# A 16-expert block on one core: every other weight chunk of the expert ring is issued by ScalarE instead of SyncE

## The reference, cut to what matters

```python
gate, idx = lax.top_k(jnp.swapaxes(affinity, 1, 2), capacity)      # capacity 32
xe = jax.vmap(lambda hb, ib: hb[ib])(h, idx)
hidden = jax.nn.silu(jnp.einsum('becd,edf->becf', xe, w_gate)) * jnp.einsum('becd,edf->becf', xe, w_up)
ye = jnp.einsum('becf,efd->becd', hidden, w_down) * gate[..., None].astype(h.dtype)
```

## Time and profile before

| | |
|---|---|
| three runs, median (lowest to highest) | 1483.31 us (1483.19 to 1488.25) |
| profiled execution: its own time | 1483.69 us |
| profiled execution: span in the trace | 1482.0 us |
| busy: PE, PEld, DVE, ACT, POOL | 78%, 46%, 34%, 25%, 3% |
| mean granted TensorE clock | 0.874 of 2.4 GHz |
| bytes moved | 493.31 MB, mean 333 GB/s |
| chain that ended last | DMA 54%, PE 41%, DVE 4% |

### The profile page before, as it was taken

One profiled execution on the slowest core, in us unless ns is written; L12 is line 12 of the kernel. 1 busy time (PEld: TensorE's weight loads), 2 busy tenths in 40 slices (PEclk: granted clock), 3 DMA queues, 4 the chain that ended last, 5 costly groups with the idle time before them and its releaser, 6 DMA issues.

```text
span 1482.0 us, 19792 instructions
## 1 busy us (share of the span) xinstructions
PE 1151.1 (78%) x8185; PEld 685.5 (46%) x8185; DVE 503.4 (34%) x926; ACT 374.3 (25%) x618; POOL 41.5 (3%) x95
## 2 busy tenths in 40 slices
PE   9999999866666567567556666565666999999998
PEld 8887887321212212112112122122121788999887
DVE  6988895101101001011011010110110569665547
ACT  6658663101001000001000100000100364465434
POOL 2220120000000000000000000000000000000000
PEclk9999999987877877877787788788877999999999
DMA  8663528999999999999999999999999763555551
GB/s 305 199 251 110 193 86 351 391 426 429 425 427 428 427 429 427 428 428 428 428 429 428 429 428 427 429 427 427 429 428 428 267 213 137 177 174 196 189 186 52
DMA packets 58616, 493.31 MB, mean 333 GB/s; under 512 B 6666, under 2 KB 8260, under 8 KB 33988
## 3 DMA queue, kind: packets, MB, share of 16 engines
q1 hardware_dynamic: 57620, 491.54, 81.5%
q10 hardware_dynamic: 944, 1.05, 0.2%
HBM read 491.52 MB, written 1.05 MB: 332 GB/s over the span
## 4 chain that ended last, share of the span: by engine, by line
DMA 54%; PE 41%; DVE 4%; issue 1%; ACT 1%; DVEq 0%; POOL 0%; SPq 0%; ACTq 0%; POOLq 0%
DMA arena<-in_expert_w_down 15%; DMA arena<-in_expert_w_up 13%; PE ps L1860 13%; DMA arena<-in_expert_w_gate 12%; PE ps L1951 7%; PE ps L1865 6%; DMA ring<-in_expert_w_gate 5%; DMA ring<-in_expert_w_down 5%; DMA ring<-in_expert_w_up 4%; PE ps L2307 4%; PE ps L2325 2%; DVE w_split L1145 1%; PE ps L1930 1%; PE ps L2121 1%; PE ps L2152 1%
## 5 line engine op out<-in xcount | busy, mean ns | idle before, releaser
L1145 DVE TENSOR_TENSOR w_split<-ring,w_split 128x1024 fp32r<-128x1024 f32 (+3 forms) x178 | 200.8, 1136 | 99.8 <-ACT w_split L721 98.6
L2307 PE MATMUL ps<-ring,arena 128*32 128x512 f32 x1024 | 166.8, 795 | 84.9 <-DMA ring<-in_expert_w_up 60.4
L2307 PE MATMUL ps<-arena 128*32 128x512 f32 x1024 | 161.1, 770 | 88.3 <-DMA arena<-in_expert_w_up 59.9
L721 ACT ACTIVATE w_split<-ring 128x1024 fp32r<-128x1024 f32 (+3 forms) x178 | 175.4, 990 | 186.2 <-PE ps L1865 130.1
L1596 DVE TENSOR_TENSOR arena<-arena,ps 128x512 f32<-128x512 f32 x16 | 11.0, 688 | 494.2 <-PE ps L2307 494.2
L1603 DVE TENSOR_TENSOR xs<-ps,xs 128x512 f32<-128x512 f32 x64 | 39.8, 684 | 298.1 <-PE ps L2333 298.1
L2307 PEld LDWEIGHTS ps<-ring,arena 128*32 128x32 f32 x1024 | 33.8, 132 | 210.3 <-DMA ring<-in_expert_w_up 102.0
L2307 PEld LDWEIGHTS ps<-arena 128*32 128x32 f32 x1024 | 33.1, 128 | 209.6 <-DMA arena<-in_expert_w_up 97.5
L1951 PE MATMUL ps<-hT_hi,w_split 128*128 128x256 f32 x608 | 111.4, 284 | 0.1
L2325 PE MATMUL ps<-arena 128*32 128x256 f32 x1056 | 81.9, 462 | 37.2 <-DMA arena<-in_expert_w_down 34.2
L2325 PE MATMUL ps<-ring,arena 128*32 128x256 f32 x928 | 77.6, 492 | 39.7 <-DMA ring<-in_expert_w_down 37.5
(11 more groups left out here) (361 smaller groups left out, 1369.8 us busy)
## 6 DMA issues: line engine op xcount, KB each, us to landing
arena<-in_expert_w_gate SPq DMA_DIRECT2D x35, 2048.0 KB, 35.8
ring<-in_expert_w_up SPq DMA_DIRECT2D x35, 2048.0 KB, 36.0
ring<-in_expert_w_gate SPq DMA_DIRECT2D x29, 2048.0 KB, 36.2
arena<-in_expert_w_up SPq DMA_DIRECT2D x29, 2048.0 KB, 37.2
arena<-in_expert_w_down SPq DMA_DIRECT2D x25, 2048.0 KB, 34.5
ring<-in_expert_w_down SPq DMA_DIRECT2D x21, 2048.0 KB, 33.8
ring<-in_w_ff SPq DMA_DIRECT2D x32, 1024.0 KB, 4.9
ring<-in_w_in SPq DMA_DIRECT2D x24, 1024.0 KB, 5.0
```

The costliest lines, as they stand in the source:

```text
L721: act.activation(w_split[:, n % WBUFS, 0, 0:cols], slot_view(slot, cols)[:, n % 2, :], ACT.Copy).then_inc(split_hi, 1)
L1145: dve.tensor_tensor(buf[:, 1, :], w, buf[:, 0, :].bitcast(F32), ALU.subtract).then_inc(split_lo, 1)
L2307: m = pe.matmul(ps[j * CAP:(j + 1) * CAP, bank, :], xe[:, kt, :], w[:, r, j * FCOL:(j + 1) * FCOL], start=kt == 0, stop=kt == KT - 1, skip ...
```

## The change

`chunk_source` and `load_chunk` move out of SP's program, and `load_chunk` gets the issuing engine as an argument. Chunks with n >= 11 and n odd are issued by ACT, all others by SP as before; SP's waits for them are the same numbers as before. Since there are 12 chunks in an expert, odd n is odd k: ACT issues k = 1, 3, 5, 7, 9 and 11 of each expert, and so both parts of each k = 11. ACT issues them between its activations: 9 and 11 of this expert after L955's copy, 1 and 3 of the next after silu, 5 and 7 of the next after the copy of the hidden, each behind a wait of its own on `chunk_used`, with the same number as SP's. ACT's loop over 8 pairs becomes one over 6; the first and the last pair stand outside it. PE, DVE and POOL are unchanged.

```diff
+        def load_chunk(engine, slot, loaded, e, k):
+
+            source = chunk_source(e, k)
+            if k < EXPERT_CHUNKS - 1:
+                engine.dma_start(slot, source).then_inc(loaded, 16)
+                return
+            engine.dma_start(slot[:, 0:TAIL], source[:, 0:TAIL]).then_inc(loaded, 16)
+            engine.dma_start(slot[:, TAIL:WIDE], source[:, TAIL:WIDE]).then_inc(tail_loaded, 16)
+
+        def from_scalar(n):
+
+            return n >= SLOTS and n % 2 == 1
...
-            for n in T1_ORDER[2:] + tuple(range(SLOTS, PAIR * EXPERT_CHUNKS)):
+            for n in T1_ORDER[2:] + tuple(n for n in range(SLOTS, PAIR * EXPERT_CHUNKS) if not from_scalar(n)):
                 load_freed(n)
             with sp.Fori(1, EXPERTS // PAIR) as pair_i:
                 for n in range(PAIR * EXPERT_CHUNKS):
-                    sp.wait_ge(chunk_used, PAIR * EXPERT_CHUNKS * pair_i + n + 2)
-                    load_chunk(wide_slots[turn(n)], slot_loaded[turn(n)], pair_i * PAIR + n // EXPERT_CHUNKS, n % EXPERT_CHUNKS)
+                    if n % 2 == 0:
+                        sp.wait_ge(chunk_used, PAIR * EXPERT_CHUNKS * pair_i + n + 2)
+                        load_chunk(sp, wide_slots[turn(n)], slot_loaded[turn(n)], pair_i * PAIR + n // EXPERT_CHUNKS,
+                                   n % EXPERT_CHUNKS)
...
-            with act.Fori(0, EXPERTS // PAIR) as pair_i:
+
+            def load_odd(e, j_e, k, ahead, first):
+
+                n = EXPERT_CHUNKS * (j_e + ahead) + k
+                if first and n < SLOTS:
+                    return
+                act.wait_ge(chunk_used, slot_free(n) if first else EXPERT_CHUNKS * (e + ahead) + k + 2)
+                load_chunk(act, wide_slots[turn(n)], slot_loaded[turn(n)], e + ahead, k)
+
+            def expert(e, j_e, first=False, last=False):
+
+                act.wait_ge(scat_done, e + 2)
+                act.wait_ge(e_scatter, e + 1)
+                act.activation(scat, ps[:, 3, 256:512], ACT.Copy).then_inc(scat_ready, 1)
+                for k in (9, 11):
+                    load_odd(e, j_e, k, 0, first)
+                act.wait_ge(chunk_used, EXPERT_CHUNKS * e + T1_RELEASES + IN_CHUNKS)
+                act.wait_ge(hid_ready, e + 1)
+                act.activation(hid_g, ps[:, 0, :], ACT.Silu).then_inc(silu_done, 1)
+                if not last:
+                    for k in (1, 3):
+                        load_odd(e, j_e, k, 1, first)
+                act.wait_ge(hidT_done, e + 2)
+                act.activation(hidT, ps[:, 2, :].rearrange("p (c t) -> p c t", c=4), ACT.Copy).then_inc(hidT_ready, 1)
+                if not last:
+                    for k in (5, 7):
+                        load_odd(e, j_e, k, 1, first)
+                act.wait_ge(chunk_used, EXPERT_CHUNKS * e + T1_RELEASES + EXPERT_CHUNKS)
+                act.activation(ye, ps[:, 3, 0:DCOL], ACT.Copy).then_inc(ye_ready, 1)
+
+            for e in range(PAIR):
+                expert(e, e, first=True)
+            with act.Fori(1, EXPERTS // PAIR - 1) as pair_i:
                 for j_e in range(PAIR):
...
+                    expert(pair_i * PAIR + j_e, j_e)
+            for e in range(EXPERTS - PAIR, EXPERTS):
+                expert(e, e % PAIR, last=e == EXPERTS - 1)
```

More of the change, by code:

```diff
@@ L434, in hybrid_blocks, with chunk_source @@
         ENDS += [(len(CORNERS) - 1, CORNERS[-1][1], D - 512 + c, 256) for c in (0, 256)]
+        def chunk_source(e, k):
+            if k < 2 * IN_CHUNKS:
+                c = k % IN_CHUNKS
+                w = t["expert_w_gate" if k < IN_CHUNKS else "expert_w_up"][0, e]
+                return w[c * P * IN_ROWS:(c + 1) * P * IN_ROWS, :].rearrange("(p r) f -> p (r f)", r=IN_ROWS)
+            c = k - 2 * IN_CHUNKS
+            w = t["expert_w_down"][0, e]
+            return w[c * P * OUT_ROWS:(c + 1) * P * OUT_ROWS, :].rearrange("(p r) d -> p (r d)", r=OUT_ROWS)
+        def load_chunk(engine, slot, loaded, e, k):
[7 more added lines that the diff above has]
+            return n >= SLOTS and n % 2 == 1
         block = ctx.enter_context(nc.Block())
@@ L481, in _ @@
                               ).then_inc(small_loaded, 16)
[L482 to L490, removed]
             load(DENSE_SLOTS)
@@ L498, in _ @@
             sp.dma_start(router[:, :, :], t["router_w"][0].rearrange("(k p) e -> p k e", p=P)).then_inc(small_loaded, 16)
[L499 to L506, removed]
             def load_expert(n):
                 slot, loaded = expert_slot(n)
-                load_chunk(slot, loaded, n // EXPERT_CHUNKS, n % EXPERT_CHUNKS)
+                load_chunk(sp, slot, loaded, n // EXPERT_CHUNKS, n % EXPERT_CHUNKS)
             def load_freed(n):
@@ L949, in _ @@
             act.sem_inc(ye_ready, 1)
-            with act.Fori(0, EXPERTS // PAIR) as pair_i:
-                for j_e in range(PAIR):
[L952 to L962, removed]
+            def load_odd(e, j_e, k, ahead, first):
[4 more added lines that the diff above has]
+                load_chunk(act, wide_slots[turn(n)], slot_loaded[turn(n)], e + ahead, k)
```

## The result

The changed kernel takes 1488.17 us (median of 20 runs, 1485.81 to 1495.66) against 1483.80 us (20 runs): ratio 1.0027, 95% interval 1.0018 to 1.0035, so 4.0 us more (2.7 to 5.2). That is a small loss: the interval leaves out 1, and it lies inside the 0.5% that the prediction called no change. 1487.3 had been forecast.

What follows compares the result with a forecast made beforehand. The prediction took the full DMA engines (428 GB/s) to bound the experts' stretch. Its terms, 0 + 0 + 0 + 4 us, gave 1487.3 us on the median of the runs, range 1480 to 1496.

Steps and rivals of the forecast that it cites:

- Rate with two rings: Expert stretch: engines alternate pieces between rings, rate stays 428 GB/s, 0 us; ends 422 and 436, +12.7 and -16.4 us.
- rivals 1 and 3: Expert stretch: two big-piece streams disturb each other, 1500 us, chance 0.12; or hide piece overhead, 1471 us, chance 0.07.
- rival 2: End of experts: rings served in groups of pieces, last tail lands at 1164.1, total 1489 us; chance 0.12.
- Issue time on ACT: ACT's loads before its activations: each delays silu or L962's copy by 0.4 to 1.2 us, hidden by slack; counted 0.
- Waits on ACT, loads 13 and 17: ACT's queue: waiting loads hold nothing up; 13 and 17 issue after activations, but chunks in flight prevent a gap; 0.
- The even ring's lead: Across experts: k = 11's smaller pieces let SP's even chunks gain a chunk per expert until its four slots fill.
- full lead: Last expert: 188 and 190 land before 187, which lands at 1149.04 instead of 1139.25; the end comes 4.7 us later.
- half a lead: Last expert: 187 lands some 2.4 us earlier, the tail's landing near 1162 sets the end, about +3 us.
- The end: Handover from last expert to second block: PE ends chunk 191 later, between 1 and 5 us; 4 us taken.
- rival 4: Last expert: PE, after standing still, is granted 1.2 GHz instead of 2.4; 10 us in all, 1493 us; chance 0.05.
- With none, +1 to +2.5: Last expert without any lead: 191 shares with at most 5 us of dense pieces or of 190, +1 to +2.5 us.

Runs made afterwards that it cites:

- e1: Changed kernel with all chunks of the last two experts issued by SP again; 1483.55 us, ratio 0.9989 to the kernel before.
- e4: Changed kernel with each k = 11 chunk loaded in one transfer instead of two; 1485.76 us, ratio 1.0011 to the kernel before.
- e2: Changed kernel with parity swapped: ACT issues even chunks, SP odd ones and both parts of k = 11; 1489.05 us, ratio 1.0030 to the kernel before.
- e3: Changed kernel with parity alternating: ACT issues odd chunks of odd experts, even chunks of even experts; 1487.25 us, ratio 1.0017 to the kernel before.
- e9: Changed kernel with ACT issuing odd chunks only in the last two experts, SP all earlier ones; 1488.43 us, ratio 1.0026 to the kernel before.
- b4: Kernel before the change, with each k = 11 chunk loaded in one transfer; 1483.40 us, ratio 0.9991 to the unedited kernel before.
- e10: Repeat, on another chip, of the changed kernel with SP issuing the last two experts' chunks; 1483.58 us, ratio 0.9996 to the kernel before.
- e5: Changed kernel with the second block's dense chunks held back until the last expert chunk's tail landed; 1489.98 us, ratio 1.0034 to the kernel before.

## Why the prediction was right

*Rate with two rings:* taken as 428, measured 428. The ends 422 and 436 were not needed, and rivals 1 and 3 fall. The argument from 32 small pieces that took 19.5 us held: turns go by pieces (shown under rival 2), and a turn costs nothing. The Trainium skill says of the same ("DMA: Bandwidth & Descriptors", section "Issuing engines are not separate DMA queues") that transfers from several engines run on the same 16 engines and save only the time of issuing; the trace agrees, 428 and 428.

*Issue time on ACT:* taken as 0.41 to 0.59 us, most issues took 0.34, and where two stand before the activation it starts 0.9 us after the first of them, but not on the path. Here silu stands behind both parts of k = 11:

```profile
664.41 0.34 ACTq L452 DMA_DIRECT2D arena<-in_expert_w_down  x1
664.91 0.34 ACTq L453 DMA_DIRECT2D arena<-in_expert_w_down  x1
665.35 0.60 ACT L975 ACTIVATE arena<-ps 128x512 f32<-128x512 f32 x1 [8.79 <-PE ps L2338]
```

PE's wait for the last copy of an expert grew from 8.1 us in 14 experts, 0.6 at the longest, to 14.2 and 1.0. Counted 0, and e1, which keeps this in 14 experts, is no slower: 0.

*Waits on ACT, loads 13 and 17:* counted 0; the DMA share is 0.99 from 270 to 275 us and 1.01 from 275 to 280 in the changed kernel:

```profile
270.00:275.00 5.00, 5.00 (x52) 1.51 (x48) 0.00 (x0) 0.66 (x2) 0.00 (x0) 1.00 0.99 408
275.00:280.00 5.00, 4.82 (x48) 1.22 (x40) 0.12 (x1) 0.00 (x0) 0.00 (x0) 1.00 1.01 425
```

*The even ring's lead:* right in cause (e4, e2) and direction, too large in size. With a full lead 188 and 190 would have landed before 187; only 188 had, and 190 landed 7.4 us after it. A full lead would have put PE's start on 187 at 1149.0 on the clock of before; it came at 1146.96 - 1.82 = 1145.1, 5.9 us late instead of 9.8, some 60% of it. In e2 the lead was nearly full, 9.6, and there the sum for a full lead held: +4.7 forecast, +4.6 measured. (For half a lead the prediction had 187 "some 2.4 us earlier"; half of 9.8 is 4.9, and the full lead's term was off by 3.9.)

*The end:* forecast +4.7 with a full lead, +4 taken, +4.0 measured, and the closeness is partly luck. The DMA side came as worked out: 191's last part was forecast at 1161.5, and landed at 897.7 after the first row, 1161.8 on the clock of before. With the lead as it was, that landing would have set the end, by this estimate near the +3 that the prediction had for half a lead. But PE did 188 and 189 at the lower granted clock (0.58 from 1151 to 1160 us): 6.17 us from 1153.28 to the small matmuls at 1159.45, where 3.44 had been put in, 2.7 us more, and the transposes before them took another 0.4. So two errors cancel: 3.9 us less from the lead, 3.1 more from PE. The clock is a part of rival 4. It came after the wait of 5.54 us before 187; but e2 waited 4.81 there and had the full clock again for 188 and 189, so the wait alone does not decide it. "With none, +1 to +2.5" was the weak estimate: e3 shows 3.4, of which 1.7 are 190 at the lower clock, e9 2.7, e4 0.9 by its trace and 2.4 by its median.

*Rival 2* (turns by groups) falls by two things on record. It had 191's last part land at 1164.1 on the clock of before, where single pieces gave 1161.5. Here is that part in the changed kernel, landed at 1163.6, which is 1161.8 on the clock of before:

```profile
L453 ACTq DMA_DIRECT2D arena<-in_expert_w_down x1: 455/455/455, 1136.7 to 1136.7; - x1
...
DMA to landing us min/median/max: 26.9/26.9/26.9
```

And the traces hold every piece with its queue, start and duration. I put them in sequences, one for each DMA engine, each piece behind the one that had just ended. In e4, between 400 and 1100 us, 99.6% of some 20,500 steps then go to the other ring, and no stretch on one ring is longer than three pieces. In the changed kernel there are 148 longer stretches, up to 20 pieces, and 145 of them are ACT's: SP's ring had run dry, as the prediction's lead needs. In e2 they are SP's. The 9 to 17 at a time, for which the prediction cites the Trainium skill at this rival, do not show here. *Rival 4* alone had 6 us of its own; some 3 came.

## What to carry to other kernels

Where the DMA engines are full, a second issuing ring moves no more bytes; it only changes the order in which they land, and the order matters where the stretch ends. Two rings that take turns by pieces give more of the engines to the ring with the larger pieces, so a split transfer on one ring lets the other run ahead. Equal pieces cure the lead but not the loss (e4): the rings carry the last two chunks beside each other, so the first of the two lands late (190 by 2.7 us in e4 against b4). If loads must be spread, put the last ones before a handover, with what follows them, on one ring (e1, e10). And compare landings before uses: here they repeated to 0.3 us, while the granted clock moved the uses by 1 to 2.

## What the runs showed of the hardware

Each ring's share follows the size of its pieces, not the engine that issues: with the split transfer on ACT, SP's gate and up chunks landed after 18 to 22 us and ACT's after 31 to 37 in the rows shown, with it on SP 36 to 38 and 24 to 26, and without it both after 36. With a lead, PE gets its chunks in pairs and was granted less clock over the middle 700 us, 0.74 to 0.75 (changed, e1, e2, e5, e10) instead of 0.78 to 0.79 in all others, e4 among them, where the pieces were equal:

```profile
400.00:1100.00 700.00, 440.84 (x3616) 149.22 (x3616) 57.83 (x132) 23.52 (x48) 0.00 (x0) 0.79 1.01 428
```

The time between the first instruction and the experts differed by 3.9 us between two profiles of one program, as much as the whole effect; only a row inside each trace to measure from, beside twenty runs, made it readable.
